# One stretch of a fused transformer kernel: x's first half is scaled in the step of conditioning unit 7, and units 8 to 15 stand one tile later

## The chip, the core and the metric

The kernel runs on one core of a Trainium2 chip. TensorE multiplies, VectorE and ScalarE do elementwise work, GpSimd helps, and SyncE and ScalarE issue the transfers from the chip's memory; sixteen DMA engines carry them. The metric is the device time of one launch in microseconds (us), the median of three runs. All times below are in us from the start of the profiled execution unless said otherwise.

## What is computed

Two transformer blocks follow each other on x (512 positions, width 2048). The stretch of this study is the start of the first one:

```python
c_act = jax.nn.silu(c)
for l in range(DEPTH):
    mod = c_act @ w_ada[l] + b_ada[l]
    shift, scale, gate = jnp.split(mod, 3, axis=-1)
    h = _rms(x, norm_g[l]) * (1.0 + scale[:, None, :]) + shift[:, None, :]
    proj = h @ w_in[l]
...
m_k, m_v = jnp.split(rmsnorm(mem, mem_norm_g[l]) @ w_mem_kv[l], 2, axis=-1)
```

`mod` is the conditioning: a vector c (2048 numbers) through a matrix of 2048 by 6144, of which shift and scale (the first 4096 columns) are wanted before h exists. `h` is x, divided by the root of its mean square, then scaled and shifted for each feature. `proj` is a large product in single precision; the kernel does it with three matmuls for each pair of operands, on a high part and a remainder of either (whi, wlo for the weights, Hhi, Hlo for h). The keys and values of the second block's memory attention (m_k, m_v) depend on nothing of x and are worked out first, mixed in with the conditioning.

## The kernel before

**Layout.** Features lie on the 128 partitions, so x and h are 16 pieces of 128x512 each. Pieces 0 to 7 are the first half (LOW), 8 to 15 the second (HIGH). A weight item is a 128x1024 load of 512 KB that serves eight pieces: half a tile of w_in. Each item passes through a ring of three buffers: a load into wraw, the high part whi made by ScalarE (L1106), the remainder wlo made by VectorE for the first 24 items (L1550), by GpSimd afterwards (L2113).

**Order.** `in_order` walks once over the whole program, and each engine's program is written out by that same walk; every engine executes its own list strictly in order, with semaphores between them. At the start it goes through the list START: `m0` to `m15` are the sixteen steps of the memory product (L733 to L735; items 0 to 15), `a0` to `a8` are units of the conditioning, `s0` and `s1` turn the conditioning's sums into columns (L763). Units are counted from 0.

**A conditioning unit** is four loads of w_ada (512 KB each, L2262, issued by SyncE) and sixteen narrow matmuls (L700). There are sixteen units in four chunks of four; all add up in the same two PSUM banks, 6 and 7 (bO and bV), and after the last unit of a chunk ScalarE copies the sum out (L1182, semaphore adr). The loads have eight places, two units: the loads of unit q go out once unit q-2 is consumed (semaphore adq in `sync_program`'s `setup`). Before unit 11's loads stands a small load of masks.

**x.** ScalarE computes 1/rms of x in step m13 (L1171, L1173; semaphore xr). VectorE multiplies each piece of x by it: `normed(x)` does four pieces (L1571). For the first half it is called in the steps m14 and m15, for the second in the steps of units 9 and 10. `gain(0)` (L1585 to L1593) then makes the scale and shift columns from s1's result, and `h_put(LOW)` does for each of eight pieces: scale and shift (VectorE, L1601), high part (ScalarE, L1216), remainder (VectorE, L1636). `gain(1)` and `h_put(HIGH)` do the same after s2 and s3.

**Begun tiles.** The table BEGUN starts eight tiles of w_in with the first half of h, each (tile, bank, units): the units are done first, then the half tile of 24 matmuls (L795 to L797) into that bank. The kernel thereby has work for TensorE while the conditioning's second half comes in. Tile 32, the last, needs bank 6 and stands behind s2, s3 and `gain(1)`. Tile 40 goes into bank 7, which is free only once ScalarE has copied the last chunk's sum: its first matmul waits for adr to be 4. Tile 48 is item 16, tile 41 item 17, and so on to tile 32, item 23.

ScalarE issues the loads of items up to 25, each in the step of the item four ahead of it; SyncE those from item 26 on, behind all the loads of w_ada.

Of the kernel before, what the change touches and what calls it, by code (L numbers as in the profile page):

```python
# [31 lines left out]
def _columns():  # L32
    at = 0
    for name, n in (("ident", 128), ("causal", 128), ("norm_g", 16), ("b_ada", 48),
# [18 lines left out]
PLACES = 8  # L53

START = [(x[0], int(x[1:])) for x in ("m0 m1 m2 a0 m3 m4 a1 m5 m6 a2 m7 a3 m8 m9 a4 m10 s0 m11 a5 m12 a6 m13 a7 "
                                      "m14 s1 m15 a8").split()]


BEGUN = ((48, 3, (9,)), (41, 2, (10,)), (56, 4, (11,)), (33, 5, (12,)), (49, 1, (13,)), (57, 0, (14, 15)), (40, 7, ()),
         (32, 6, ()))  # L60

GATE_SLOTS = 6

# [20 lines left out]
def weights():  # L84
# [3 lines left out]
    def plan(name, first, count, cols=1024):  # L88
        out.extend((name, i, 0, cols) for i in range(first, first + count))
# [11 lines left out]
    plan("w_mem", 0, KT)  # L101
    begun = [tile for tile, _, _ in BEGUN]
    for tile in begun:
# [345 lines left out]
def in_order(beat, do):  # L449
# [35 lines left out]
    do["h_put"](LOW)  # L485
    for tile, bank, fours in BEGUN:
        for i in fours:
            do["ada"](i)
        if tile == BEGUN[-1][0]:
            do["sums"](2)  # L490
# [3 lines left out]
        do["part"]("h", LOW, bank, True, False)  # L494
    begun = {tile: bank for tile, bank, _ in BEGUN}
    beat.add("slow", do["gates"](0))
# [1005 lines left out]
def vector_program(nc, M, S, beat):  # L1502
# [42 lines left out]
    def rest_of(j):  # L1545

        if j < FIRST_RESTS:
            b, w = j % NRING, ITEMS[j][3]
            dve.wait_ge(S.hi, j + 1)
            e.tensor_tensor(M.wlo[b][:, 0:w], M.wraw[b][:, 0:w], M.whi[b][:, 0:w].bitcast(F32),  # L1550
                            ALU.subtract).then_inc(S.lo)

    def mem_rest(k):
        dve.wait_ge(S.phi, k + 1)
        e.scalar_tensor_tensor(out=M.pair["mem"][1][k], in0=M.memt[k], scalar=M.c("mem_g", k, 1),
                               in1=M.pair["mem"][0][k].bitcast(F32), op0=ALU.mult, op1=ALU.subtract).then_inc(S.plv)
        n.up("plv")

    def mem(k):
        rest_of(beat.item + 2)  # L1560
        if k < 6:
            mem_rest(2 * k + 4)
            mem_rest(2 * k + 5)
        if k in (14, 15):
            normed(4 * k - 56)
        beat.done("mem", [])

    def normed(x):
        for x in range(x, x + 4):
            dve.wait_ge(S.xr, 2)  # L1570
            e.tensor_tensor(M.y[x], M.y[x], M.xr, ALU.mult).then_inc(S.xn)  # L1571

    def ada(q):
        if q in (9, 10):
            normed(4 * q - 28)
        if q == 13:
            dve.wait_ge(S.mask, 16)
            e.tensor_copy(M.mk, M.masks_in.bitcast(I32)).then_inc(S.mask8)
# [513 lines left out]
    def nothing(*at):  # L2092
        pass

    in_order(beat, dict(
        setup=setup, mem=mem, mem_kv=mem_kv, mem_turn=lambda: rest(2), ada=ada, sums=nothing, gain=gain, h_put=h_put,
        gates=gates, hg=hg, attend=attend, window=window, put=put, x_load=nothing, h2=h2, index=index, topk=topk, mix_load=nothing, out_load=nothing, end=nothing,
        part=part, out=out, posts=dict(
# [386 lines left out]
```

## Time and profile before

| | us |
|---|---|
| median of three runs | 2669.47 (2667.93 to 2669.85) |
| the profiled execution, its own time | 2672.98 |
| its span, first to last instruction | 2671.7 |
| TensorE busy in it | 2635.5 (99%) |
| TensorE's share of the chain that ended last | 95% |
| mean granted clock | 0.995 |

The profiled execution is 3.5 us above the median of the runs; 1.3 us of its time lie outside its span. TensorE is busy nearly throughout, and where it stands still, or runs at a lower clock, is mostly in the first 170 us. The page's first part gives the busy time of each engine; the chain of waits gives, step by step in order of time, what released what; the timeline lists instructions with the idle time before them in square brackets; the view by stretch gives TensorE's busy time, its granted clock (1.00 is 2.4 GHz, 0.50 is 1.2 GHz) and the traffic of the DMA engines. A matmul's duration in the timeline holds its tail, which lies over the next one: the step from one start to the next is what a stream of them costs.

### The profile page before, as it was taken

The page shows a single profiled execution, that of the slowest core. Times are in us where ns is not written, and L with a number is a line of the kernel's source. Part 1 is how long each engine was busy: PE and PEld are TensorE (multiplying, and loading weights), DVE is VectorE, ACT ScalarE, POOL GpSimd, SP SyncE. Part 2 cuts the span into 40 slices and gives each one's busy share as a digit, 9 for nine tenths or more (in the row PEclk, how much of TensorE's full clock was granted, in tenths as well). Part 3 has the DMA queues.
Part 4 walks back from the last instruction along what each step waited for, and adds up shares of the span by engine and source line. Part 5 has one row for each costly group of instructions (what it writes and reads, how often), then busy time and mean ns, then how long its engine had stood idle before and what let it go on. Part 6 is the DMA issues. An engine that isn't in the chain of part 4 may idle for free.

```text
span 2671.7 us, 34011 instructions
## 1 busy us (share of the span) xinstructions
PE 2635.5 (99%) x13854; PEld 2113.7 (79%) x13854; DVE 969.0 (36%) x1584; ACT 1094.4 (41%) x1781; POOL 1163.8 (44%) x590
## 2 busy tenths in 40 slices
PE   7999999999999999999999999999999999999999
PEld 4577777878888888878887777777888888888787
DVE  3535544333334231244676333334332233121400
ACT  5335444434444442244444444444444444333321
POOL 0024434343444454453344444445555556544543
PEclk9999999999999999999999999999999999999999
DMA  9943233233333224422222332332333333333343
GB/s 384 347 148 104 95 104 111 80 117 116 115 115 103 89 97 157 146 91 80 87 81 77 104 96 96 102 98 97 105 113 110 112 113 116 115 117 112 132 148 107
DMA packets 102252, 322.89 MB, mean 121 GB/s; under 512 B 11473, under 2 KB 13265, under 8 KB 101585
## 3 DMA queue, kind: packets, MB, share of 16 engines
q1 hardware_dynamic: 98208, 307.06, 34.1%
q10 hardware_dynamic: 3888, 13.66, 1.3%
q8 instruction: 110, 1.80, 0.3%
q14 instruction: 46, 0.37, 0.0%
HBM read 303.90 MB, written 16.78 MB: 120 GB/s over the span
## 4 chain that ended last, share of the span: by engine, by line
PE 95%; DVE 2%; DMA 2%; ACT 1%; issue 0%; POOL 0%; SPq 0%; ACTq 0%; DVEq 0%
PE bank L795 28%; PE bank L797 27%; PE bank L796 27%; DMA TA<-in_w_ada 2%; PE bank L1002 1%; PE bank L991 1%; PE bank L922 1%; PE bank L700 1%; DVE Hlo L1636 1%; PE bank L985 1%; PE bank L956 1%; PE bank L1037 1%; PE bank L1051 0%; PE bank L862 0%; PE bank L733 0%; PE bank L848 0%
## 5 line engine op out<-in xcount | busy, mean ns | idle before, releaser
L2113 POOL TENSOR_TENSOR wlo<-wraw,whi 128x1024 fp32r<-128x1024 f32 (+3 forms) x430 | 993.2, 2310 | 1373.2 <-ACT whi L1106 1372.8
L795 PE MATMUL bank<-Hhi,whi 128*128 128x512 f32 x2928 | 1181.9, 404 | 6.1 <-DVE TA L1689 3.5
L797 PE MATMUL bank<-Hhi,wlo 128*128 128x512 f32 x2928 | 1144.7, 391 | 0.0
L796 PE MATMUL bank<-Hlo,whi 128*128 128x512 f32 x2928 | 1144.5, 391 | 0.0
L1106 ACT ACTIVATE whi<-wraw 128x1024 fp32r<-128x1024 f32 (+3 forms) x454 | 457.3, 1008 | 663.8 <-PE bank L797 636.9
L795 PEld LDWEIGHTS bank<-Hhi,whi 128*128 128x128 f32 x2928 | 551.3, 188 | 141.4 <-issue 21.1
L797 PEld LDWEIGHTS bank<-Hhi,wlo 128*128 128x128 f32 x2928 | 550.8, 188 | 118.3
L796 PEld LDWEIGHTS bank<-Hlo,whi 128*128 128x128 f32 x2928 | 551.8, 188 | 111.0 <-issue 2.4
L795 PE MATMUL bank<-Ohi,whi 128*128 128x512 f32 x320 | 128.1, 400 | 0.9 <-DVE TA L1668 0.9
L797 PE MATMUL bank<-Ohi,wlo 128*128 128x512 f32 x320 | 124.8, 390 | 0.0
L796 PE MATMUL bank<-Olo,whi 128*128 128x512 f32 x320 | 124.7, 390 | 0.0
L1668 DVE TENSOR_TENSOR TA<-bank,rows 128x512 f32<-128x512 f32 x48 | 33.1, 690 | 223.7 <-PE bank L797 223.7
L1230 ACT ACTIVATE TA<-bank 128x512 f32<-128x512 f32 x64 | 38.0, 593 | 144.3 <-PE bank L797 144.3
L1780 DVE TENSOR_TENSOR TR<-TA,TR 128x512 fp32r<-128x512 f32 x38 | 60.6, 1595 | 100.1 <-ACT TR L1308 100.1
L1322 ACT ACTIVATE TA<-bank,par 128x512 f32<-128x512 f32 x39 | 26.9, 690 | 120.0 <-PE bank L849 119.9
L1727 DVE SCALAR_TENSOR_TENSOR TA<-TA,par 128x512 f32<-128x512 f32 x48 | 48.5, 1011 | 72.0 <-ACT TA L1258 69.5
L795 PEld LDWEIGHTS bank<-Ohi,whi 128*128 128x128 f32 x320 | 60.1, 188 | 14.7 <-issue 2.8
L796 PEld LDWEIGHTS bank<-Olo,whi 128*128 128x128 f32 x320 | 60.2, 188 | 13.1 <-issue 1.2
L797 PEld LDWEIGHTS bank<-Ohi,wlo 128*128 128x128 f32 x320 | 60.0, 188 | 12.7
L1668 DVE TENSOR_TENSOR Y<-bank,rows 128x512 f32<-128x512 f32 x45 | 30.9, 687 | 96.3 <-PE bank L797 89.8
L1699 DVE TENSOR_TENSOR TA<-bank,TA 128x512 f32<-128x512 f32 x16 | 11.1, 692 | 148.7 <-PE bank L797 148.7
L1258 ACT ACTIVATE TA<-TA 128x512 f32<-128x512 f32 x96 | 60.7, 633 | 3.1
(261 smaller groups left out, 2427.4 us busy)
## 6 DMA issues: line engine op xcount, KB each, us to landing
wraw<-in_w_in SPq DMA_DIRECT2D x304, 512.0 KB, 3.5
TA<-in_w_ada SPq DMA_DIRECT2D x64, 512.0 KB, 8.3
wraw<-in_w_out SPq DMA_DIRECT2D x32, 512.0 KB, 3.5
wraw<-in_w_o SPq DMA_DIRECT2D x32, 512.0 KB, 3.5
wraw<-in_w_mem ACTq DMA_DIRECT2D x16, 512.0 KB, 7.1
Y<-in_w_ada SPq DMA_DIRECT2D x16, 512.0 KB, 4.5
first<-in_w_ada SPq DMA_DIRECT2D x16, 512.0 KB, 4.5
tmp_mgs<-TA SPq DMA_DIRECT2D x32, 256.0 KB, 2.1
```

The source lines that it names most:

```text
L700: m = e.matmul(out[32 * g:32 * g + 32, :], w, x, start=start, stop=stop, skip_group_check=True)
L795: e.matmul(out, hi[:, c], xhi[k], start=first and j == 0, stop=False)
L796: e.matmul(out, hi[:, c], xlo[k], start=False, stop=False)
L797: m = e.matmul(out, lo[:, c], xhi[k], start=False, stop=last and end)
L1106: e.activation(M.whi[b][:, 0:w], M.wraw[b][:, 0:w], ACT.Copy).then_inc(S.hi)
L1230: e.activation(M.dst(kind, *at), src, ACT.Copy).then_inc(S.eva)
L1258: e.activation(M.t1, M.t1, ACT.Ln, bias=1.0).then_inc(S.sg)
L1322: e.activation(W["R"], M.bST, ACT.Ln, scale=1.0 / k, bias=M.eps).then_inc(S.ln)
L1668: e.tensor_tensor(dst, src, M.rows, ALU.mult).then_inc(S.evd)
L1727: e.scalar_tensor_tensor(out=M.t2, in0=x, scalar=bias, in1=M.t1, op0=ALU.min, op1=ALU.subtract).then_inc(S.t2)
L1780: e.tensor_tensor(M.sql, M.W2["SQ"], M.sqh.bitcast(F32), ALU.subtract).then_inc(S.sql)
L2113: e.tensor_tensor(M.wlo[b][:, 0:w], M.wraw[b][:, 0:w], M.whi[b][:, 0:w].bitcast(F32), ALU.subtract).then_inc(S.lo)
```

## The change

`normed` for the first half leaves the steps m14 and m15 and goes into the step of unit 7, which stands ahead of m14. In the tables, unit 8 leaves START and stands behind tile 48, and each later unit stands one tile later: 9 behind 41, 10 behind 56, 11 behind 33, 12 and 13 behind 49, 14 and 15 behind 57 and so directly ahead of tile 40.

```diff
 START = [(x[0], int(x[1:])) for x in ("m0 m1 m2 a0 m3 m4 a1 m5 m6 a2 m7 a3 m8 m9 a4 m10 s0 m11 a5 m12 a6 m13 a7 "
-                                      "m14 s1 m15 a8").split()]
+                                      "m14 s1 m15").split()]
...
-BEGUN = ((48, 3, (9,)), (41, 2, (10,)), (56, 4, (11,)), (33, 5, (12,)), (49, 1, (13,)), (57, 0, (14, 15)), (40, 7, ()),
-         (32, 6, ()))
+BEGUN = ((48, 3, ()), (41, 2, (8,)), (56, 4, (9,)), (33, 5, (10,)), (49, 1, (11,)), (57, 0, (12, 13)),
+         (40, 7, (14, 15)), (32, 6, ()))
...
-        if k in (14, 15):
-            normed(4 * k - 56)
         beat.done("mem", [])
...
     def ada(q):
+        if q == 7:
+            normed(0)
+            normed(4)
         if q in (9, 10):
             normed(4 * q - 28)
```

The instructions of each engine are the same in number; only their order differs. (One added line shifts the numbers behind it by one: L1571 becomes L1569, L1585 becomes L1586, L1601 becomes L1602.)

VectorE, from the remainders of the memory product's weights to the columns of `gain(0)`; before:

```order
L1550 TENSOR_TENSOR wlo<-wraw,whi 128x1024 [waits s_hi] x9
L1571 TENSOR_TENSOR Y<-Y,rows 128x512 [waits s_xr]
L1571 TENSOR_TENSOR Y<-Y,rows 128x512 x3
L1550 TENSOR_TENSOR wlo<-wraw,whi 128x1024 [waits s_hi]
L1571 TENSOR_TENSOR Y<-Y,rows 128x512 x4
L1585 TENSOR_TENSOR par<-bank,cst 128x8 [waits s_adc]
```

and of the changed kernel:

```order
L1550 TENSOR_TENSOR wlo<-wraw,whi 128x1024 [waits s_hi] x8
L1569 TENSOR_TENSOR Y<-Y,rows 128x512 [waits s_xr]
L1569 TENSOR_TENSOR Y<-Y,rows 128x512 x7
L1550 TENSOR_TENSOR wlo<-wraw,whi 128x1024 [waits s_hi] x2
L1586 TENSOR_TENSOR par<-bank,cst 128x8 [waits s_adc]
```

The eight multiplications by 1/rms now stand ahead of the last two remainders (items 16 and 17), and nothing is left between item 17's remainder and `gain(0)`.

TensorE, from the last matmuls of m15 to the first of tile 48 (s_ada are the places of w_ada, s_plv counts VectorE's remainders of h); before:

```order
L735 MATMUL bank<-wlo,Hhi 128x512
L700 MATMUL bank<-TA 32x512 [waits s_ada2,s_ada3,s_ada1,s_ada0]
L700 MATMUL bank<-TA 32x512 x7
L700 MATMUL bank<-TA 32x512 [waits s_ada6,s_ada7,s_ada5,s_ada4]
L700 MATMUL bank<-TA 32x512 x7
L795 MATMUL bank<-Hhi,whi 128x512 [waits s_plv,s_xr,s_lo]
```

and of the changed kernel:

```order
L734 MATMUL bank<-whi,Hlo 128x512
L735 MATMUL bank<-wlo,Hhi 128x512
L795 MATMUL bank<-Hhi,whi 128x512 [waits s_plv,s_xr,s_lo]
L796 MATMUL bank<-Hlo,whi 128x512
L797 MATMUL bank<-Hhi,wlo 128x512
```

Units 8 and 9 are gone from between m15 and tile 48.

TensorE at the start of tile 40, whose first matmul waits for s_adr; before (tile 57's last matmuls, then tile 40):

```order
L795 MATMUL bank<-Hhi,whi 128x512
L796 MATMUL bank<-Hlo,whi 128x512
L797 MATMUL bank<-Hhi,wlo 128x512
L795 MATMUL bank<-Hhi,whi 128x512 [waits s_adr,s_lo]
L796 MATMUL bank<-Hlo,whi 128x512
```

and of the changed kernel:

```order
L797 MATMUL bank<-Hhi,wlo 128x512
L700 MATMUL bank<-TA 32x512 [waits s_ada2,s_ada3,s_ada1,s_ada0]
L700 MATMUL bank<-TA 32x512 x7
L700 MATMUL bank<-TA 32x512 [waits s_ada6,s_ada7,s_ada5,s_ada4]
L700 MATMUL bank<-TA 32x512 x7
L795 MATMUL bank<-Hhi,whi 128x512 [waits s_adr,s_lo]
```

Units 14 and 15 moved from ahead of tile 57 to directly ahead of tile 40.

## Rows read from the trace of the kernel before

**Rows 1.** The page: busy time, and the chain of waits by engine.

```profile
PE 2635.5 (99%) x13854; PEld 2113.7 (79%) x13854; DVE 969.0 (36%) x1584; ACT 1094.4 (41%) x1781; POOL 1163.8 (44%) x590
...
PE 95%; DVE 2%; DMA 2%; ACT 1%; issue 0%; POOL 0%; SPq 0%; ACTq 0%; DVEq 0%
```

**Rows 2.** Timeline of TensorE: start, us, instruction, [idle before <- releaser].

```profile
91.13 2.68 PE L700 MATMUL bank<-TA 128*32 128x512 f32 x16 [2.85 <-DMA TA<-in_w_ada]
...
97.44 1.84 PE L763 MATMUL bank<-par,first 128*128 128x1 f32 x16
...
102.09 3.64 PE L700 MATMUL bank<-TA 128*32 128x512 f32 x32
105.71 0.47 PE L795 MATMUL bank<-Hhi,whi 128*128 128x512 f32 x1
...
113.65 1.92 PE L700 MATMUL bank<-TA 128*32 128x512 f32 x16
...
121.17 1.92 PE L700 MATMUL bank<-TA 128*32 128x512 f32 x16
```

**Rows 3.** Timeline of VectorE, from item 16's remainder to h's first half.

```profile
95.86 1.23 DVE L1550 TENSOR_TENSOR wlo<-wraw,whi 128x1024 fp32r<-128x1024 f32 x1 [10.83 <-ACT whi L1106]
97.00 2.49 DVE L1571 TENSOR_TENSOR Y<-Y,rows 128x512 f32<-128x512 f32 x4
99.41 1.22 DVE L1550 TENSOR_TENSOR wlo<-wraw,whi 128x1024 fp32r<-128x1024 f32 x1
100.54 2.49 DVE L1571 TENSOR_TENSOR Y<-Y,rows 128x512 f32<-128x512 f32 x4
102.95 0.23 DVE L1585 TENSOR_TENSOR par<-bank,cst 128x8 f32<-128x8 f32 x2
...
104.87 0.69 DVE L1636 TENSOR_TENSOR Hlo<-Y,Hhi 128x512 fp32r<-128x512 f32 x1 [0.24 <-ACT Hhi L1216]
```

**Rows 4.** Timeline of ScalarE: 1/rms, item 17's high part, the last chunk's copy.

```profile
86.28 0.63 ACT L1173 ACTIVATE rows<-rows 128x512 f32<-128x512 f32 x1
...
97.69 1.06 ACT L1106 ACTIVATE whi<-wraw 128x1024 fp32r<-128x1024 f32 x1 [1.87 <-PE bank L735]
...
149.79 1.03 ACT L1182 ACTIVATE first<-bank 128x1024 f32<-128x1024 f32 x1 [12.28 <-PE bank L700]
```

**Rows 5.** Timeline of TensorE around the last two units.

```profile
143.85 1.92 PE L700 MATMUL bank<-TA 128*32 128x512 f32 x16
147.81 1.92 PE L700 MATMUL bank<-TA 128*32 128x512 f32 x16 [2.04 <-DMA TA<-in_w_ada]
...
155.24 0.39 PE L795 MATMUL bank<-Hhi,whi 128*128 128x512 f32 x1
...
160.68 3.93 PE L763 MATMUL bank<-par,first 128*128 128x1 f32 x32
```

**Rows 6.** Timeline of SyncE's queue: the issues for units 10 and 15.

```profile
104.08 1.75 SPq L2262 DMA_DIRECT2D TA<-in_w_ada  x4
...
138.27 1.84 SPq L2262 DMA_DIRECT2D TA<-in_w_ada  x4
```

**Rows 7.** Chain of waits: the last load of unit 15, issue to landing.

```profile
139.59 8.08 DMA TA<-in_w_ada
```

**Rows 8.** By stretch: TensorE busy, granted clock, DMA share, GB/s.

```profile
90.00:95.00 5.00, 3.87 (x19) 0.72 0.64 256
...
105.00:110.00 5.00, 4.69 (x21) 1.00 1.01 356
...
140.00:145.00 5.00, 5.00 (x30) 1.00 0.96 338
145.00:150.00 5.00, 2.96 (x25) 1.00 0.29 118
```

**Rows 9.** By stretch of 2 us: length, granted clock, DMA share, GB/s.

```profile
99.00:101.00 2.00, 1.00 1.03 420
...
103.00:105.00 2.00, 1.00 0.04 16
```

## The prediction

> **What bounds the kernel now.** The page first: TensorE is busy 99% of the span and holds 95% of the chain that ended last [rows 1]. So the change is worth what it does to TensorE's stops and to its clock between 94 and 165 us; nothing else moves. Then the timelines of that stretch, to see what each stop waits for. TensorE's matmuls follow one another there but for three things. It stands 2.85 us before unit 7, and its clock falls afterwards [rows 2, 8]. Tile 48 goes at the pace of h's pieces: its 24 matmuls take from 105.71 to 113.65, 7.9 us, where tile 40 takes 5.4 (155.24 to 160.68) [rows 2, 5]. And it stands 2.04 us before unit 15, whose last load landed at 147.67 [rows 5, 7]. The DMA engines are nearly full from 105 to 145 us, eight stretches at 338 to 411 GB/s with a mean of 368, and almost idle at 103 to 105, when both units in the places were waiting to be consumed [rows 8, 9].
>
> **VectorE's part.** 1/rms of x is there at 86.91 [rows 4]. Four multiplications take 2.41 us (97.00 to 99.41), so eight run from 86.9 to 91.7, inside the 10.83 us in which VectorE waits for item 16's high part. That wait hides them; item 16's remainder starts at 95.86 as before [rows 3]. Item 17's high part ends at 98.75 [rows 4], its remainder takes 1.22 and ends at 100.0, and s1 is over at 99.28 [rows 2]. So `gain(0)` starts at 100.0, not 102.95: **2.95 us earlier**. If the cover were gone it would cost at most the 4.8 us it now removes; nothing points to that.
>
> **TensorE at tile 48.** From `gain(0)` to tile 48's first matmul are 2.76 us (102.95 to 105.71), to its end 10.70 (113.65) [rows 2, 3]. With the new start these are 102.7 and 110.7. But m15 still ends at 102.09, and units 8 and 9, which filled 102.09 to 105.7, are no longer there: TensorE stands 0.6 us. The slow pace of tile 48 (VectorE's two operations for a piece) stays whole. After tile 48 and two units the old order is at 113.65, the new one would be at 110.7 + 3.7 = 114.4. **Cost +0.7 us**; the earlier start is spent on replacing the two units. Bounds: 0.4 to 1.0, as the 0.6 is a difference of short handovers.
>
> **The units behind it.** Unit 8 now ends at 112.55. A tile with a unit takes 7.52 us (113.65 to 121.17) [rows 2], so units 9, 10, 11 and 12 end at 120.1, 127.6, 135.1 and 142.65, unit 13 at 144.5, tile 57 (5.5 us) at 150.0, unit 14 at 151.9. TensorE wants unit 15 then, which is the old 145.77 with tile 57 and the 0.7 added.
>
> **The loads.** Unit 10's loads went out at 104.08 [rows 6]; now they wait for unit 8, until 112.5. The DMA engines lie idle for that long, and bytes not moved then have to be moved later. In the middle it does not matter: 2.1 MB of a unit and 0.5 MB of an item in 7.5 us need 350 GB/s, just about what the engines give. At the end it does. Unit 14's loads go out at 142.65 (unit 12 consumed), unit 15's at 144.5: eight loads of 0.524 MB, 4.19 MB, which at 368 GB/s take 11.4 us. The first microsecond after an issue into idle engines brings next to nothing (16 GB/s over 103 to 105, issue at 104.08 [rows 6, 9]), and some 0.3 us of unit 13 and of the items is left over. So the last load lands at 142.65 + 0.9 + 11.4 + 0.3 = 155.3. As a check, before it took 9.4 us from unit 15's first issue to its last landing (138.27 to 147.67) with most of a unit ahead of it [rows 6, 7]; now nearly the whole of unit 14 is ahead, 1.9 us earlier. TensorE's waits for data are then 155.3 - 151.9 = 3.4 us (perhaps 0.4 of it already at unit 13, issued at 135.1 and wanted at 142.65), where 2.04 were: **+1.4 us**. Bounds: at 420 GB/s (rows 9) the landing is 153.6, -0.3; at 338 GB/s (last full stretch of rows 8), with 0.6 left over, 156.6, +2.7. I take the mean rate, since the same kinds of load run in the same mixture.
>
> The Trainium skill, page "DMA: Bandwidth & Descriptors", section "Bandwidth", says that for loads from the chip's memory the memory's side binds at about 358 GB/s for a core, and shows 425 GB/s for a lone core beside it. By 358 the landing would be 155.6 and the term +1.7; by 425 it would be 153.5 and -0.4. The row of 420 GB/s speaks for the second as a peak, the mean of 368 lies near the first.
>
> **Tile 40 behind unit 15.** Before, ScalarE copied the last chunk's sum out of banks 6 and 7 while TensorE did tile 57: 149.79 to 150.82, where tile 40 came at 155.24 [rows 4, 5]. Tile 57 is the cover, and it is gone: now tile 40 follows unit 15 at once and needs bank 7. TensorE stands from the unit's end to the copy's end and a handover, 1.1 to 1.2 us. **+1.15 us**. Behind the waiting matmul stand tile 40, s2 and s3, `gain(1)`, tile 32 and all that follows; nothing fills the hole.
>
> **The clock.** After the 2.85 us before unit 7 the granted clock averaged 0.72 over 90 to 95, part of it at 1.2 GHz; the unit took 2.68 us instead of 1.92 and m14 3.6 (93.81 to 97.44) where m15 took 2.8 (99.28 to 102.09): 0.8 + 0.8, 1.6 us [rows 2, 8]. After the 2.04 us before unit 15 it stayed at 1.00 [rows 5, 8]. Here I expect about 3 us before unit 15, near the first case, and a second stop of 1.15 behind its 1.9 us. I take a fall, at 1.4 us, as some of it lies over the second stop: **+1.4 us**. Bounds: 0, and 2.7 if half of tile 40 (5.4 us at full speed) runs at half speed.
>
> The Trainium skill, page "TensorE: Matmul & The Clock Gate", section "A second HAM failure mode: psum-queue depth-cycling", says that short idle spells between groups of matmuls, often enough repeated, also make the clock go down and up. By that rule the fall comes even where each stop is shorter than the one before unit 7, and the sum is 4.6; by the 2.04 us stop, which cost nothing, it is 3.2.
>
> **Sum:** 0.7 + 1.4 + 1.15 + 1.4 = 4.65 us. The profiled execution (2672.98) would become 2677.6; it lies 3.5 above the median, so the median becomes 2669.47 + 4.65 = 2674.1. Moving the copy of unit 11's chunk and the loads of items 20 to 26 costs nothing: each is ready 5 us or more before its use, under tiles of 5.4 us.
>
> **Rivals.**
> - *The clock holds.* For it speaks the 2.04 us stop, and that the wait may be split over units 13 and 15, each part shorter than 2.85. 3.25 us more: 2672.7. Chance 30%.
> - *Slower by more than 0.2%, through the DMA engines.* They run at 338 GB/s or less in the last two units; the end lands at 156.6 instead of 155.3, +1.3 on the sum, and the longer stop keeps the clock low into tile 40, +0.9 more: +6.8, 2676.3. It decides from a landing at about 156, as 0.2% is 5.3 us. For it: four stretches of the eight are below 360. Against: the engines are emptier than before when unit 14 begins. Chance 15%.
> - *The change does not do what it says.* `gain(0)` is held at 102.95 by something that the rows do not show, such as a slower remainder. TensorE then stands 3.6 us at tile 48 instead of 0.6: +3.0 on the sum, 2677.1. Chance 4%.
> - *The holes are filled.* Unit 15 lands in time, the 2.04 us vanish, and 0.7 + 1.15 remain: 2669.3. It needs 4.19 MB in 151.9 - 143.5 = 8.4 us, 500 GB/s, and rows 9 show 420 at best. Chance 6%.
>
> **How the numbers follow.** The forecast has 45%, with a range of its own of 2673.0 to 2675.4. The range 2670.8 to 2676.8 leaves out the last two rivals and the outer edges, under 20%. A measurement of this kernel can tell about 0.2%, 5.3 us, from no change: slower means above 2674.8. That holds the third and second rival (19%) and about a fifth of the forecast (9%): slower 28%. Faster has 2%, a part of the last rival. Within 0.2% the rest: 70%.
>
> **What would show it.** In the changed kernel's timelines: eight multiplications at about 87 to 91.7, `gain(0)` near 100.0, tile 48 from 102.7 to 110.7, unit 10's loads near 112.5 with the DMA engines idle from 103, TensorE's last wait for w_ada at about 152 lasting about 3 us, 1.1 us before tile 40 released by ScalarE's copy, a granted clock of 0.5 within 152 to 160, and the s2, s3 group at about 165 instead of 160.7. The prediction is wrong if tile 48 starts before 102.1, if unit 15 waits less than 2 us, if tile 40 follows without a stop, or if a stretch behind 170 us moves by anything but the shift.

## The result, and the profile after

The changed kernel takes 2674.85 us, the median of 13 runs (2673.33 to 2680.56); the kernel before, run beside it, takes 2669.85 (13 runs, 2667.53 to 2674.9). The ratio is 1.0019 with a 95% interval of 1.0011 to 1.0028: 5.0 us slower, a real difference, and inside the 0.2% that the prediction calls no change. Forecast were +4.65 us and 2674.1. The sum came out right. How it is made up did not, and that is what the experiments are about.

The page of the changed kernel, busy times and the chain of waits, to be laid beside [rows 1]: nothing moved but 1% of the chain, from TensorE.

```profile
PE 2635.7 (99%) x13854; PEld 2112.1 (79%) x13854; DVE 969.2 (36%) x1584; ACT 1094.5 (41%) x1781; POOL 1163.6 (44%) x590
...
PE 94%; DMA 2%; DVE 2%; ACT 1%; SPq 0%; POOL 0%; issue 0%; DVEq 0%; ACTq 0%
```

Timeline of TensorE in the changed kernel, the rows that answer to [rows 2, 5]: s1, tile 48, units 8, 12, 13, units 14 and 15 in one row, tile 40, s2 with s3.

```profile
93.88 1.84 PE L763 MATMUL bank<-par,first 128*128 128x1 f32 x16
...
99.12 0.47 PE L795 MATMUL bank<-Hhi,whi 128*128 128x512 f32 x1 [0.52 <-DVE Hlo L1637]
...
107.07 1.92 PE L700 MATMUL bank<-TA 128*32 128x512 f32 x16
...
137.28 1.92 PE L700 MATMUL bank<-TA 128*32 128x512 f32 x16
144.45 3.64 PE L700 MATMUL bank<-TA 128*32 128x512 f32 x16 [5.24 <-DMA TA<-in_w_ada]
...
154.60 3.64 PE L700 MATMUL bank<-TA 128*32 128x512 f32 x32
159.48 0.47 PE L795 MATMUL bank<-Hhi,whi 128*128 128x512 f32 x1 [1.24 <-ACT first L1182]
...
165.05 3.63 PE L763 MATMUL bank<-par,first 128*128 128x1 f32 x32
```

Three stops stand in square brackets. Those before tile 48 (0.52) and before tile 40 (1.24, released by ScalarE's copy) are where and as long as the prediction has them. The third is not: 5.24 us before unit 13, none before units 14 and 15. Unit 13 itself takes 3.64 us where unit 12 takes 1.92, so half speed.

Timeline of VectorE in the changed kernel, which answers to [rows 3]: the eight multiplications, the remainders of items 16 and 17, `gain(0)`.

```profile
87.77 4.91 DVE L1569 TENSOR_TENSOR Y<-Y,rows 128x512 f32<-128x512 f32 x8 [1.92 <-ACT rows L1173]
93.16 1.23 DVE L1550 TENSOR_TENSOR wlo<-wraw,whi 128x1024 fp32r<-128x1024 f32 x1 [0.47 <-ACT whi L1106]
95.22 1.23 DVE L1550 TENSOR_TENSOR wlo<-wraw,whi 128x1024 fp32r<-128x1024 f32 x1 [0.84 <-ACT whi L1106]
96.36 0.23 DVE L1586 TENSOR_TENSOR par<-bank,cst 128x8 f32<-128x8 f32 x2
```

The eight multiplications fit in front of item 16's remainder, which still waits 0.47 us for ScalarE behind them: their cover holds.

By stretch, TensorE of the changed kernel: length, busy time, granted clock, share and GB/s of the DMA engines. Beside [rows 8, 9]: idle DMA engines where they had been full, engines that are not full from 123 to 133 either, and a low clock behind unit 13.

```profile
103.00:108.00 5.00, 4.71 (x25) 1.00 0.37 105
108.00:113.00 5.00, 5.00 (x30) 1.00 0.59 185
113.00:118.00 5.00, 5.00 (x31) 1.00 1.03 413
...
123.00:128.00 5.00, 5.00 (x29) 1.00 0.85 319
128.00:133.00 5.00, 5.00 (x30) 1.00 0.78 292
133.00:138.00 5.00, 5.00 (x28) 1.00 0.94 371
138.00:143.00 5.00, 1.21 (x12) 1.00 1.01 385
143.00:148.00 5.00, 3.55 (x16) 0.51 0.69 274
```

### The profile page after: what moved, and what is told of

It reads as the page before. It is cut to its first block, busy times and chain, and to the rows that moved or that the text cites. A ratio compares the mean times of both kernels' runs of the same rounds, so it can differ in the third digit from the quotient of the medians.

```text
span 2674.8 us, 34011 instructions
## 1 busy us (share of the span) xinstructions
PE 2635.7 (99%) x13854; PEld 2112.1 (79%) x13854; DVE 969.2 (36%) x1584; ACT 1094.5 (41%) x1781; POOL 1163.6 (44%) x590
## 4 chain that ended last, share of the span: by engine, by line
PE 94%; DMA 2%; DVE 2%; ACT 1%; SPq 0%; POOL 0%; issue 0%; DVEq 0%; ACTq 0%
PE bank L795 28%; PE bank L797 27%; PE bank L796 27%; DMA TA<-in_w_ada 2%; PE bank L1002 1%; PE bank L991 1%; PE bank L700 1%; PE bank L922 1%; DVE Hlo L1637 1%; PE bank L985 1%; PE bank L956 1%; PE bank L1037 1%; PE bank L1051 0%; PE bank L862 0%; PE bank L848 0%; PE bank L1029 0%
## 5 line engine op out<-in xcount | busy, mean ns | idle before, releaser
L796 PEld LDWEIGHTS bank<-Olo,whi 128*128 128x128 f32 x320 | 60.1, 188 | 13.1 <-issue 1.2
L1700 DVE TENSOR_TENSOR TA<-bank,TA 128x512 f32<-128x512 f32 x16 | 11.1, 692 | 148.7 <-PE bank L797 148.7
```

The source lines that it names most:

```text
L796: e.matmul(out, hi[:, c], xlo[k], start=False, stop=False)
```

## The experiments

Two measures are used. The first is the median against that of the kernel before on the same chip (2669.85, 2670.53, 2670.38 and 2671.29 us in the four sets of runs), with its ratio and 95% interval. The second is read from the profile: TensorE's s1 group, its s2 group, and the stretch between them, in which all of the change to TensorE's order lies. The second is needed since the runs of one kernel spread over 5 us and more; the last section shows one source of that. It has a spread of its own, one profile each: 1.5 us between the two profiles of the kernel before, 3.5 between e1 and e12, which are one kernel.

| kernel | s1 at | s2 at | stretch | TensorE's stops in it, us | median against before |
|---|---|---|---|---|---|
| before, the profile of the prediction | 97.44 | 160.68 | 63.24 | unit 15 2.04 | |
| before again (e7) | 92.41 | 157.18 | 64.77 | unit 9 1.91, unit 15 2.65 | |
| changed | 93.88 | 165.05 | 71.17 | 0.52, unit 13 5.24, copy 1.24 | +5.0 |
| changed again (e9) | 92.86 | 162.78 | 69.92 | 0.53, unit 13 3.72, unit 15 1.03, copy 1.23 | |
| VectorE's part alone (e1) | 93.65 | 157.15 | 63.50 | unit 9 1.73, unit 15 2.63 | -2.9 |
| the same again (e12) | 93.44 | 160.44 | 67.00 | unit 9 2.00, unit 10 1.44, unit 15 3.10 | -1.4 |
| tables alone (e2) | 93.86 | 168.21 | 74.35 | tile 48 4.40, unit 13 2.21, unit 15 3.17, copy 1.23 | +8.4 |
| before, small loads (e3) | 94.32 | 156.18 | 61.86 | unit 9 2.62 | -3.9 |
| changed, small loads (e4) | 93.14 | 156.24 | 63.10 | 0.52, copy 1.24 | -2.7 |
| e1 with unit 8 forward (e6) | 93.09 | 159.00 | 65.91 | unit 9 2.77, unit 15 2.33 | -1.5 |
| e4 with tile 57 as cover (e8) | 96.29 | 159.86 | 63.57 | 0.52, unit 14 1.91 | -3.3 |
| e1 with unit 15 behind tile 57 (e10) | 93.59 | 157.71 | 64.12 | unit 9 3.53, copy 1.24 | -2.5 |
| e4 with units in pairs (e11) | 92.73 | 154.05 | 61.32 | 0.53 | -6.4 |

### The two parts apart

First VectorE's part alone, with the tables as before.

```diff
-        if k in (14, 15):
-            normed(4 * k - 56)
...
+        if q == 7:
+            normed(0)
+            normed(4)
```

> The kernel before with VectorE's part alone: the first half is multiplied by 1/rms in the step of unit 7, the tables stay as they were, so units 8 and 9 still fill TensorE while gain(0) runs. Theory A (the loads of w_ada bound the stretch from unit 10 on): h's pieces are about 3 us ahead and tile 48 takes 5.5 us instead of 7.9, but unit 15's data land hardly earlier, so its wait grows from 2.0 to about 4 us and the time falls by 0.5 us only (2669.3, at most 2.4 less). Rival B (TensorE and VectorE's pace bound it): the whole 2.4 us are gained, 2667.4, and unit 15's wait stays at 2.

2667.59 (11 runs) against 2670.53: 0.9990, 0.9981 to 0.9999. The time is nearer to theory B; unit 15's wait, 2.63 us, lies between the two. The same kernel once more, beside the later versions:

> VectorE's part alone once more, beside the version with unit 15 moved, on the same chip: from s1 to s2 63.5 us again (64.8 in the kernel before), unit 9 waits 1.7 and unit 15 2.6. Theory A: what it gains on the kernel before is tile 48 at 5.6 us instead of 6.7, 1.1 us; the 2.9 us between the medians of the first comparison were partly the chance of the clock later in the program. So 2669.0, 1.1 under the kernel before. Rival: 2667.6 again, 2.9 under it.

2669.86 (12 runs) against 2671.29: 0.9997, 0.9989 to 1.0006. The gain, 1.4 us, is near theory A; the stretch is not, 67.0 us instead of 63.5, with a stop at unit 10 that e1 does not have and a longer one at unit 15. Taken together the part is worth 1 to 3 us, at the edge of what can be told; the second interval alone includes no change.

Then the tables alone, with `normed` left in the steps m14 and m15.

```diff
-                                      "m14 s1 m15 a8").split()]
+                                      "m14 s1 m15").split()]
...
-BEGUN = ((48, 3, (9,)), (41, 2, (10,)), (56, 4, (11,)), (33, 5, (12,)), (49, 1, (13,)), (57, 0, (14, 15)), (40, 7, ()),
-         (32, 6, ()))
+BEGUN = ((48, 3, ()), (41, 2, (8,)), (56, 4, (9,)), (33, 5, (10,)), (49, 1, (11,)), (57, 0, (12, 13)),
+         (40, 7, (14, 15)), (32, 6, ()))
```

> The changed kernel with VectorE's part undone: the tables' shift alone. Theory A: gain(0) starts 3 us later than in the changed kernel, TensorE stands about 3.6 us before tile 48 instead of 0.5, and unit 8 and with it all later loads shift by 3 us, so the time is 3 us above the changed kernel: 2677.9. Rival B (the loads alone decide, or VectorE's part is hidden anyway): the stop before tile 48 is paid out of the wait before unit 13 or 15, and the time is the changed kernel's, 2674.9.

2678.89 (7 runs) against 2670.53: 1.0026, 1.0015 to 1.0037. That is theory A, with about 1 us more: `gain(0)` comes 3.9 us later than in the changed kernel, not 3. Timelines of this kernel: first VectorE, at s1's result, then TensorE at tile 48 and the last pair of units.

```profile
97.82 2.49 DVE L1571 TENSOR_TENSOR Y<-Y,rows 128x512 f32<-128x512 f32 x4
100.23 0.23 DVE L1585 TENSOR_TENSOR par<-bank,cst 128x8 f32<-128x8 f32 x2
```

```profile
102.98 0.66 PE L795 MATMUL bank<-Hhi,whi 128*128 128x512 f32 x1 [4.40 <-DVE Hlo L1636]
...
145.26 1.93 PE L700 MATMUL bank<-TA 128*32 128x512 f32 x16 [2.21 <-DMA TA<-in_w_ada]
...
157.93 3.48 PE L700 MATMUL bank<-TA 128*32 128x512 f32 x16 [3.17 <-DMA TA<-in_w_ada]
162.65 0.47 PE L795 MATMUL bank<-Hhi,whi 128*128 128x512 f32 x1 [1.23 <-ACT first L1182]
```

`gain(0)` starts 6.37 us behind s1 here (100.23 - 93.86) and 2.48 behind it in the changed kernel (96.36 - 93.88): the multiplications, moved, bring it 3.89 us forward, and the stop before tile 48 shrinks by 3.88. So the tables by themselves cost 8.4 us and VectorE's part gives 3.4 of them back (8.4 - 5.0, from two sets of runs). In the old order the same part is worth only 1.4 to 2.9, since unit 9 stands ahead of tile 48 and its data come at 101 to 102 either way.

### The kernel before and the changed one, profiled again

> The kernel before, profiled once more, unchanged: the first profile had a stop of 2.85 us at unit 7, the profiles of four variants that are equal up to there had 0.6 to 2.2. Theory A: unit 7 waits 1 to 2 us, TensorE arrives at units 8 and 9 some 3 us earlier and unit 9 has to wait for its data 1.5 to 2.5 us, as in the variants; unit 15 waits about 2. Rival: unit 9 goes without a wait, as in the first profile.

2669.62 us, one run. Unit 9 waits as theory A has it; unit 7 waits less than it says, 0.22 us, and unit 15 more. Timeline of TensorE in it, at s1 and at units 8, 9 and 15.

```profile
92.41 1.84 PE L763 MATMUL bank<-par,first 128*128 128x1 f32 x16
97.07 1.92 PE L700 MATMUL bank<-TA 128*32 128x512 f32 x16
100.90 1.92 PE L700 MATMUL bank<-TA 128*32 128x512 f32 x16 [1.91 <-DMA TA<-in_w_ada]
...
144.30 1.92 PE L700 MATMUL bank<-TA 128*32 128x512 f32 x16 [2.65 <-DMA TA<-in_w_ada]
```

The profile on which the prediction rests is the odd one out. There unit 7 stood 2.85 us and then ran at a low clock [rows 2, 8], so s1 came at 97.44 and unit 9's data were there in time. Here unit 7 stands 0.22, s1 comes at 92.41, and the wait is before unit 9. Of the twelve profiles taken since, eleven have s1 between 92.4 and 94.4; e8 has 96.29, behind a stop of 2.71 before unit 7.

> The changed kernel, profiled once more, unchanged: the first profile had 5.2 us at unit 13 and none at unit 15, where the prediction had 0.4 and 3.0. Theory A: 5.2 was one slow part of a load; this time about 1 us at unit 13 and 2 to 3 at unit 15, as in the tables' shift alone (2.2 and 3.2), and 1.2 before tile 40. Rival: unit 13 waits 5 us again, which the order of the loads would then cause.

2675.04 us, one run. Timeline of TensorE in it, at unit 13, unit 15 and tile 40.

```profile
141.92 3.60 PE L700 MATMUL bank<-TA 128*32 128x512 f32 x16 [3.72 <-DMA TA<-in_w_ada]
...
154.07 1.92 PE L700 MATMUL bank<-TA 128*32 128x512 f32 x16 [1.03 <-DMA TA<-in_w_ada]
157.22 0.47 PE L795 MATMUL bank<-Hhi,whi 128*128 128x512 f32 x1 [1.23 <-ACT first L1182]
```

Neither expectation is met: unit 13 waits 3.72 us, not 1 and not 5, and unit 15 1.03, not 2 to 3. The pattern of the first profile repeats, and the total of the stops for loads does so more closely than its parts: 5.24 us at unit 13, or 3.72 + 1.03 = 4.75 over both.

### The loads taken out of it

Three theories stood against each other. At one end: the cost is in the order of TensorE's work, whatever the loads do (5.0 us would be left without them). At the other: it is all in the loads, with the clock behind them (0 would be left). Between them: 1.85 us are TensorE's order. Both kernels got the same cut, to 64 of 1024 columns for units 10 to 15; these units then multiply columns that were not loaded.

```diff
-            e.dma_start(M.ada_slot[a % PLACES], io["w_ada"][CHUNKS[a // 16], a % 16]).then_inc(S.ada[a % PLACES], 16)
+            w = 1024 if a < 40 else 64
+            e.dma_start(M.ada_slot[a % PLACES][:, 0:w], io["w_ada"][CHUNKS[a // 16], a % 16, :, 0:w]).then_inc(S.ada[a % PLACES], 16)
```

> The kernel before, with the loads of units 10 to 15 cut to 64 of 1024 columns (the rest of each place keeps old data, so the gate of the second half is not computed rightly): no wait for these loads is left. Theory A: the 2.0 us before unit 15 go and nothing else: 2667.8. Rival: the loads also hold up other things there (the items' loads); then more than 2.0 goes.

> The changed kernel with the same cut of the loads of units 10 to 15. What it keeps over the same cut of the kernel before is the cost of TensorE's order alone. Theory A: 0.7 us before tile 48 and 1.15 us before tile 40, together 1.85 over that one (about 2669.7); the other 3 us of the 5.0 lost are waits for loads and the clock that falls behind them. Rival B (all is in the loads): equal to the kernel before with the same cut. Rival C (all is in TensorE's order): 5.0 above it.

2666.59 (11 runs; 0.9983, 0.9973 to 0.9992) for the kernel before so cut, 2667.86 (11 runs; 0.9987, 0.9978 to 0.9996) for the changed one. The difference of the medians is 1.27 us, which their overlapping intervals alone would not secure; between the two stretches it is 1.24. Both ends fall; the theory between them is nearest, 0.6 us too high. The kernel before gains 3.9 us by the small loads, not the 2.0 of its theory A. TensorE in the kernel before so cut, at unit 9, then in the changed one so cut, at tile 48 and tile 40:

```profile
103.52 1.92 PE L700 MATMUL bank<-TA 128*32 128x512 f32 x16 [2.62 <-DMA TA<-in_w_ada]
```

```profile
98.39 0.47 PE L795 MATMUL bank<-Hhi,whi 128*128 128x512 f32 x1 [0.52 <-DVE Hlo L1637]
...
150.67 0.47 PE L795 MATMUL bank<-Hhi,whi 128*128 128x512 f32 x1 [1.24 <-ACT first L1182]
```

About 1.3 us of the 5.0 are TensorE's order, the other 3.7 are gone with the loads: their stops and the clock behind these. The 1.3 are a net, and that they equal the copy's 1.24 is chance. The new order pays 0.52 before tile 48, 1.93 for its slower pace (7.96 us instead of 6.03) and 1.24 before tile 40, and saves the 2.62 us before unit 9, whose loads are not among those cut: 1.07, and small differences in the other tiles.

### ScalarE's copy

The 1.24 us before tile 40 can be tested with the small loads, where nothing else stands in the way. Tile 57 as cover, all four last units ahead of it:

```diff
-BEGUN = (..., (57, 0, (12, 13)), (40, 7, (14, 15)), ...
+BEGUN = (..., (57, 0, (12, 13, 14, 15)), (40, 7, ()), ...
```

> The changed kernel with the loads of units 10 to 15 cut to 64 of 1024 columns (the second half's gate is then not computed rightly) and with units 14 and 15 ahead of tile 57, which then lies between unit 15 and tile 40. It tells the price of tile 40's wait for ScalarE's copy: theory A 1.2 us below the same kernel with units 14 and 15 ahead of tile 40 (2667.9), so 2666.7, and no stop before tile 40 in the timeline. Rival: the stop moves elsewhere (s2 and s3, or tile 57), and the time stays.

2667.1 (11 runs), 0.9990, 0.9981 to 0.9999. The stop before tile 40 is gone, but one of 1.91 us before units 14 and 15 took its place, as even a small load has to be issued once its place is free. The rival is what happened, and that tells nothing of the copy. The same with the units in pairs, a tile between one pair and the next:

```diff
-BEGUN = (..., (33, 5, (10,)), (49, 1, (11,)), (57, 0, (12, 13)), (40, 7, (14, 15)), ...
+BEGUN = (..., (33, 5, (10, 11)), (49, 1, (12, 13)), (57, 0, (14, 15)), (40, 7, ()), ...
```

> The changed kernel with the loads of units 10 to 15 cut to 64 of 1024 columns (the second half's gate is then not computed rightly) and the units in pairs, 10 and 11 behind tile 56, 12 and 13 behind 33, 14 and 15 behind 49: tile 57 lies between unit 15 and tile 40, and a tile lies between each unit's loads and its use. Theory A: the stop of 1.24 us before tile 40 goes and none comes in its place, so s1 to s2 takes 61.9 us instead of 63.1, and the time is 2666.6. Rival: the stop moves, 63.1 and 2667.9.

2664.88 (11 runs), 0.9977, 0.9969 to 0.9986, so -6.4 us against the kernel before, where e4 has -2.7. TensorE stands 0.53 us before tile 48 and nowhere else until s2; the stretch is 61.32 us, 1.8 shorter than e4's. Of that, 1.24 are the copy. Some 0.4 of the rest are changes between unit and tile, of which e11 has fewer: two units in a row take 3.57 us there, one by one 1.86 each in e4 (0.15), and tiles 57 and 40 in a row 11.01 us, apart 5.67 and 5.57 (0.23). The last 0.2 I can't name. The stretch shows the copy's price, the medians (3.7 apart, across two chips) agree in sign.

### Other places for the units

Unit 8 forward, between s1 and m15, on top of e1:

```diff
-                                      "m14 s1 m15 a8").split()]
+                                      "m14 s1 a8 m15").split()]
```

> A version: VectorE's part kept, the tables of the kernel before, but unit 8 pulled forward, between s1 and m15. Its data are there by about 95 us, and unit 10's loads go out about 2.8 us earlier, which fills idle time of the DMA engines. Theory A (the loads bound the stretch's end, VectorE's pace its start): unit 15's wait of 2.6 us shrinks to under 1 and the time is about 2 us below VectorE's part alone (2667.6): 2665.5. Rival: unit 9's wait grows by what unit 10's loads take, or m15 behind unit 8 delays tile 48, and the time is 2667.6 or above.

2668.9 (11 runs) against 2670.38: 0.9995, 0.9986 to 1.0003. I had expected 2665.5, a miss. By stretch, TensorE of this kernel around unit 9's wait, columns as above:

```profile
97.00:99.00 2.00, 2.00 (x10) 1.00 1.01 410
99.00:101.00 2.00, 0.75 (x4) 1.00 1.03 418
101.00:103.00 2.00, 0.48 (x8) 1.00 1.02 416
```

The DMA engines are at 410 to 418 GB/s before and all through the wait. Unit 10's loads go out at 96.84 here, 3.2 to 3.5 us sooner than in e12 and e1, into engines that are full already. They land sooner (107.48; 109.06 and 110.91 in e1 and e12), but only e12 had to wait for them. Unit 9's land 0.5 us later (102.39; 101.83 and 101.88), and it waits 2.77 us here, 1.73 and 2.00 in e1 and e12. Unit 15's land no sooner than e1's (144.39; 144.14).

Unit 15 one tile later, on top of e1:

```diff
-... (57, 0, (14, 15)), (40, 7, ()), ...
+... (57, 0, (14,)), (40, 7, (15,)), ...
```

> A version: VectorE's part with the tables of the kernel before, except that unit 15 alone moves behind tile 57, directly ahead of tile 40. It sets the two prices against each other: the wait for unit 15's data (2.6 us in two profiles, landing at 144.2) is covered by tile 57's 5.5 us, and tile 40 has to wait 1.24 us for ScalarE's copy of the last chunk. Theory A: -2.6 + 1.2 = -1.4 us against VectorE's part alone, from s1 to s2 62.1 us instead of 63.5; no wait for w_ada behind unit 9. Rival: unit 15's loads or the copy come later by as much, and nothing is gained.

2668.78 (11 runs) against 2671.29: 0.9989, 0.9981 to 0.9998. Timeline of TensorE at unit 15 and at tile 40 in this kernel:

```profile
149.02 1.92 PE L700 MATMUL bank<-TA 128*32 128x512 f32 x16
152.18 0.47 PE L795 MATMUL bank<-Hhi,whi 128*128 128x512 f32 x1 [1.24 <-ACT first L1182]
```

Unit 15's stop of 2.6 to 3.1 us is covered by tile 57, and the copy's 1.24 has lost its cover. On paper that gains 1.4 us, and 1.1 are measured against e12 on the same chip, which the intervals of the two (0.9989 to 1.0006 for e12) don't tell apart; in this profile unit 9 stood 3.53 us, which hides it from the stretch. This and e1's kernel are the best with full loads that came out of the study, at 0.9989 and at 0.9990 and 0.9997 of the kernel before. Neither is clearly better than the other.

## Why the prediction was right, and where it was not

**VectorE's part: the direction right, the size short.** Forecast were eight multiplications under the wait of VectorE for item 16's high part and `gain(0)` 2.95 us earlier. They run at 87.77 to 92.68, ahead of item 16's remainder, and `gain(0)` comes 3.89 us earlier by the comparison of e2 with the changed kernel. In the profile before, item 17's high part came at 98.75, so its remainder could start only 0.6 us earlier, and four multiplications (2.4 us) lay behind it [rows 3, 4]. In e2 the same remainder starts at 96.69, in the changed kernel at 95.22, 1.47 earlier; with the 2.4 that is 3.9. The rival by which `gain(0)` stays where it was is false; what it would have cost is e2's 4.40 us before tile 48, near the 3.6 that the prediction gives it.

**TensorE at tile 48: right.** 0.6 us were forecast, 0.52 and 0.53 measured, with the slow pace of the tile whole: 99.12 to 107.07 is 7.95 us, where 7.9 were forecast. What the prediction does not have is that an ordinary execution of the kernel before waits there too, 1.91 us for unit 9, and then does the tile in 6.74 (102.75 to 109.49), as it comes late enough to find the first four pieces of h ready one after the other. The new order is freed of that wait and pays for it with the slower tile: 0.53 + 1.21 - 1.91 is -0.2 us, for a forecast of +0.7.

**The idle DMA engines: they idle as forecast.** Unit 10's loads go out at 109.06, right behind unit 8 (108.92); forecast was the same event at 112.5, the whole being 3.6 us earlier by s1. From 103 to 108 the engines move 105 GB/s where the kernel before moved 414 in its second profile. That this idle time has to be paid for later is not shown. From 123 to 133 the engines of the changed kernel are not full, 319 and 292 GB/s at shares of 0.85 and 0.78 (290 and 272 in e9), so most of what was put off had been moved before unit 13's loads went out at 131.7.

**The waits for loads: where they come from right in kind, the term mis-sized.** I gave unit 15 3.0 us and unit 13 0.4, 3.4 in all. Measured are 5.24 and 4.75, most of it at unit 13. Unit 15's last load was to land at 155.3 and did at 155.8 and 153.9, but that is no confirmation: counted from s1 57.9 us were forecast and 61.9 and 61.1 are measured, as unit 13's stop holds back the issue of unit 15's loads. Issue and landing of unit 13's four loads in the changed kernel:

```profile
L2263 SPq DMA_DIRECT2D TA<-in_w_ada x4: 328/449/697, 131.7 to 133.1; - x4
...
DMA to landing us min/median/max: 7.7/9.0/11.2
```

and of unit 15's in the second profile of the kernel before:

```profile
L2262 SPq DMA_DIRECT2D TA<-in_w_ada x4: 328/468/625, 134.2 to 135.6; - x4
...
DMA to landing us min/median/max: 6.2/7.5/8.6
```

The step that failed is the 0.4. A unit that stands directly behind another gets its place free one tile and one unit before it is wanted, 7.5 us. The prediction has this figure for unit 13 (135.1 to 142.65), and five lines further the 9.4 us that unit 15 needed for the same way before. Laid side by side they say 1.9 us for unit 13, not 0.4. I took 9.4 for a special case of the end, but from first issue to last landing it is 9.4, 10.0 and 10.0 us at unit 15 of the order before (rows 6 and 7, e7, e1), 12.6, 11.1 and 9.6 at unit 13 of the new one (changed, e9, e2), and 7.7 to 14.3 over units 10 to 15 in all the profiles with full loads. What sets the second of a pair apart is not this time but the other one: a single unit has 13.1 us (unit 11 of the changed kernel, issued at 116.59 and done at 129.72), it has 7.5. The new tables have two such pairs, 12 and 13, 14 and 15. That unit 15 waits 1.03 us or not at all is no gain: TensorE is by then late enough. So the prediction's cause for the last pair, loads that go out too late for their use, holds one pair earlier; its words on bytes not moved while the engines were idle are not borne out by engines that had room again at 123 to 133. No run takes the two apart, as none with full loads has the idle time without the early pair.

The prediction's lower bound has a slip that changes nothing here: at 420 GB/s its own terms give a landing at 153.8, not 153.6. The rate of 368 GB/s that the landing rests on is near what the engines then moved: 371 over 133 to 138, 385 over 138 to 143. The Trainium skill, page "DMA: Bandwidth & Descriptors", section "Bandwidth", puts the memory's side at about 358 GB/s for a core beside 425 seen on a lone one. The full stretches shown behind the prediction lie at 371 to 418, those of [rows 8] at 338 and 356, so 358 is no ceiling in this case's trace, and the second figure is near its peaks. In the changed kernel's first profile a part of one load was late besides, as the last section shows, and no mean rate tells of that.

**Tile 40 behind unit 15: right.** Forecast 1.15 us for ScalarE's copy, measured 1.24, 1.23, 1.23, 1.24 and 1.24 in the five profiles that have unit 15 directly ahead of tile 40, and none where tile 57 stands between.

**The clock: the fall right, its place not, its size short.** It was to fall behind unit 15. It fell behind unit 13, where the stop was: granted 0.51 over 143 to 148, unit 13 at 3.64 us instead of 1.92, and the first four matmuls of tile 57 slow too (the tile takes 6.58 us, 5.66 in e9), 2.6 us in all; in e9 only unit 13 is slow, 1.7 us. Forecast were 1.4. The Trainium skill, page "TensorE: Matmul & The Clock Gate", section "A second HAM failure mode: psum-queue depth-cycling", says that short idle spells between groups of matmuls, often enough repeated, make the clock go down and up. The trace does not show that here: in tile 48, whose matmuls stand for a moment before nearly each piece of h (7.95 us for what takes 5.5), the clock stays at 1.00. Single longer stops have no firm tie to it either. Behind 2.63 and 2.65 us it stayed up (e1, e7), behind 2.33 it fell in part (e6), behind 3.10 it fell (e12), behind 3.53 it stayed up (e10). Why is open.

**Why the sum holds all the same.** Term by term, in us, with e7 as the profile of before, since both it and the changed kernel's have s1 at 92.4 to 93.9:

| term | forecast | e9 - e7 | changed - e7 |
|---|---|---|---|
| tile 48 and what stood before it | +0.7 | 0.53 + 1.21 - 1.91 = -0.2 | -0.2 |
| stops for loads behind it | +1.4 | 4.75 - 2.65 = +2.1 | 5.24 - 2.65 = +2.6 |
| the copy before tile 40 | +1.15 | +1.2 | +1.2 |
| the clock | +1.4 | +1.7 | +2.6 |
| sum | +4.65 | +4.8 | +6.2 |
| the stretch | | +5.15 | +6.40 |

The medians are 5.0 apart. So terms failed in opposite directions: the stops for loads (0.7 to 1.2 us too small) and the clock (0.3 to 1.2 too small) on one side, tile 48 (0.9 too large, the wait for unit 9 not seen) on the other. That the total came within 0.4 us of the measured one is partly luck. That the s2 group stands at 165.05, where about 165 was forecast, is luck altogether: s1 comes 3.6 us earlier than in the prediction's profile, and the stretch is 7.9 us longer than there.

**The rivals.** With the clock's fall in both profiles, *the clock holds* (2672.7) is out. *Slower through the DMA engines* (2676.3) lacks its condition: the engines ran at 371 and 385 GB/s, not at 338 or less, and unit 15 landed no later than 155.8. *The holes are filled* (2669.3) did not happen: the stops for loads grew. Of the signs of error that the prediction names, two came up, tile 48 before 102.1 and unit 15 waiting less than 2 us, both by way of the earlier s1 and of unit 13's stop. The sign on what lies behind 170 us can't be read so finely: from the s2 group's start to the end of the span are 2511.0 us in the prediction's profile, 2509.75 and 2510.9 in the two of the changed kernel, and 2508.35 in e1, with the same instructions there.

**Left open.** Why one part of a load lands so late in some executions, on which most of the difference between unit 13's waits (5.24, 3.72, 2.21) rests; when the clock falls; whether the idle time at 103 to 108 costs anything. More places for the loads, which might fill it and would give the second of a pair more time, were not tried.

## What to carry to other kernels

Where loads have two places and two consumers stand back to back, the second gets only the time of what lies between two pairs; lay the time from issue to landing of such a load (here 9.4 to 12.6 us) beside the time until it is wanted (here 7.5), for every pair and not for the last alone. A consumer that is moved back delays the loads that wait for its place. The idle time that this opens is what one sees first; here the engines had room again before the stop came (292 to 319 GB/s from 123 to 133). And one profile is one execution: before stops of 1 to 3 us are added up, a second one tells which of them are always there.

## What the runs showed of the hardware

**A load is as late as its slowest sixteenth.** Each of these loads lands in sixteen parts, as many as there are DMA engines. In the changed kernel fifteen parts of unit 13's four loads were there well before the last, and TensorE waits for the last (landing times counted from the trace, us):

```
load of unit 13                  1      2      3      4
fifteen of sixteen parts by  135.9  137.8  139.1  140.4
the sixteenth at             139.4  140.7  141.9  144.3
```

The fourth load's last part is 3.9 us behind the fifteenth, and TensorE starts 0.14 us behind it. In e9 it is 1.2 us (140.6 and 141.8), in e2 0.1 (145.0 and 145.1). An estimate from these figures: with all parts as early as the fifteenth, unit 13 would have waited 1.3, 2.5 and 2.1 us in the three, around the 1.9 that issue to landing against time of use gives. What made the one part late no run shows.

**A later stop is at times followed by a low clock, and this is one source of the runs' spread.** TensorE stands 3.46 us in each of the thirteen profiles, up to a matmul at 1814 to 1828 us, far behind the change. By stretch, second profile of the kernel before, then e1:

```profile
1815.00:1820.00 5.00, 2.84 (x7) 0.62 0.41 133
1820.00:1825.00 5.00, 5.00 (x18) 0.70 0.33 129
```

```profile
1815.00:1820.00 5.00, 2.89 (x13) 1.00 0.44 136
1820.00:1825.00 5.00, 5.00 (x24) 1.00 0.34 126
```

The same pause (2.84 and 2.89 us busy of 5), once at 0.62 and 0.70, once at full speed; e1's is the only profile of the study without a fall there. Laid matmul by matmul (counted from the trace), the way past this pause takes 2.7 us longer in the first than in e1, and 1.6 to 2.7 us longer in the other eleven; no edit touches it. It is half of what this study measures, and a reason for the second measure beside the medians.
